# Opening loads of a two-layer hybrid kernel issued on three DMA queues, and its parameter columns made two blocks later

## The reference

```python
for i in range(DEPTH):                                   # DEPTH = 2
    mod_l = split(silu(c) @ w_mod[i] + b_mod[i], 6)      # six vectors of 1024, latent
    mod_c = split(silu(c_ctx) @ w_mod[i] + b_mod[i], 6)  # the same for the context
    uc = modulated_norm(xc, norm1_w[i], mod_c[0], mod_c[1]) @ w_in[i]
    yc, ssd_ctx, ml_ctx = token_mixers(uc, p, ssd_zero, ml_zero, not last)
    ul = modulated_norm(xl, norm1_w[i], mod_l[0], mod_l[1]) @ w_in[i]
    yl, _, _ = token_mixers(ul, p, ssd_ctx, ml_ctx, True)
    xl = xl + mod_l[2] * (yl @ w_out[i])
    xl = xl + mod_l[5] * hier_moe(modulated_norm(xl, norm2_w[i], mod_l[3], mod_l[4]), p)
    # the context rows likewise, in layer 0 alone
return rmsnorm(xl, final_norm_w)
```

## Time and profile before

| what | value |
|---|---|
| median of 3 runs | 1335.11 us (1330.76 to 1339.67) |
| the profiled execution's own time | 1335.6 us |
| its span, from first to last instruction | 1333.7 us |
| mean granted TensorE clock | 0.946 of full speed |
| TensorE busy with matmuls | 1177.0 us, 88% of the span |
| VectorE, ScalarE, GpSimd busy | 605.7, 306.7, 133.2 us |
| bytes moved | 321.40 MB, 241 GB/s in the mean |

### The profile page before, as it was taken

How to read it: one execution, slowest core, us unless ns; L and a number is a source line. 1 busy time by engine, 2 the same in 40 slices (tenths; PEclk the granted TensorE clock), 3 DMA queues, 4 the chain that set the end, 5 groups by cost and what they waited for, 6 DMA issues and landing times. The chain is left out here.

```text
span 1333.7 us, 19484 instructions
## 1 busy us (share of the span) xinstructions
PE 1177.0 (88%) x7596; PEld 774.2 (58%) x7596; DVE 605.7 (45%) x1233; ACT 306.7 (23%) x623; POOL 133.2 (10%) x144
## 2 busy tenths in 40 slices
PE   6799999999899989999778689998889899988882
PEld 3444547977678754555444466466768655545551
DVE  4423996038963642343111256964294533332223
ACT  4201212265352202131111232122542200000001
POOL 0000000000000012222121100000000112222220
PEclk9899999999889989999888899998999899998997
DMA  8653333337651679999999745441574879999982
GB/s 273 191 175 96 96 111 95 93 125 232 204 192 37 248 249 384 393 387 366 386 380 377 273 144 168 128 139 50 171 254 180 352 282 387 386 387 393 403 342 114
DMA packets 146421, 321.40 MB, mean 241 GB/s; under 512 B 28217, under 2 KB 111222, under 8 KB 121368
## 3 DMA queue, kind: packets, MB, share of 16 engines
q1 hardware_dynamic: 134840, 304.08, 63.1%
q0 software_dynamic: 11392, 15.79, 3.6%
q10 hardware_dynamic: 96, 0.26, 0.0%
HBM read 320.32 MB, written 21.23 MB: 256 GB/s over the span
## 5 line engine op out<-in xcount | busy, mean ns | idle before, releaser
L649 PE MATMUL bank<-hT,ring 128*128 128x512 f32 (+1 forms) x544 | 205.7, 535 | 1.8 <-DVE hT L1772 1.8
L649 PE MATMUL bank<-ring,hT 128*128 128x256 f32 (+1 forms) x928 | 182.3, 352 | 7.1 <-DVE ysum L1776 3.6
L649 PEld LDWEIGHTS bank<-ring,hT 128*128 128x128 f32 x928 | 155.6, 195 | 26.5 <-issue 5.2
L649 PE MATMUL bank<-chain,qkT 128*64 128x256 f32 (+1 forms) x792 | 149.9, 394 | 12.7 <-DMA chain<-in_moe_w_up 5.4
L649 PEld LDWEIGHTS bank<-hT,ring 128*128 128x128 f32 x544 | 103.2, 192 | 98.0 <-issue 91.6
L1776 DVE TENSOR_TENSOR ktok<-ktok,bank 64x256 f32<-64x256 f32 x65 | 27.5, 423 | 279.7 <-ACT ktok L1390 215.8
L1390 ACT ACTIVATE ktok<-bank 64x256 f32<-64x256 f32 (+2 forms) x79 | 32.1, 407 | 349.0 <-PE bank L649 273.4
L649 PEld LDWEIGHTS bank<-chain,qkT 128*64 128x64 f32 (+1 forms) x792 | 89.1, 156 | 33.7 <-issue 12.3
L1323 POOL DMA_INDIRECT pair_rows<-hyT,ysum x65 | 65.7, 1010 | 385.8 <-ACT hyT L1390 197.9
L649 PE MATMUL bank<-ring,qkT 128*64 128x256 f32 x528 | 87.2, 404 | 11.9 <-DMA ring<-in_moe_w_up 8.1
L649 PEld LDWEIGHTS bank<-ring,qkT 128*64 128x64 f32 x528 | 53.5, 145 | 28.5 <-issue 9.7
(11 more groups left out here) (291 smaller groups left out, 1698.9 us busy)
## 6 DMA issues: line engine op xcount, KB each, us to landing
ring<-in_w_mod SPq DMA_DIRECT2D x40, 1024.0 KB
chain<-in_moe_w_up SPq DMA_DIRECT2D x23, 1024.0 KB
ring<-in_w_in SPq DMA_DIRECT2D x22, 1024.0 KB
chain<-in_moe_w_down SPq DMA_DIRECT2D x19, 1024.0 KB
chain<-in_moe_w_gate SPq DMA_DIRECT2D x19, 1024.0 KB
ring<-in_moe_w_down SPq DMA_DIRECT2D x18, 1024.0 KB
ring<-in_moe_w_up SPq DMA_DIRECT2D x17, 1024.0 KB
ring<-in_moe_w_gate SPq DMA_DIRECT2D x16, 1024.0 KB
```

What stands on the lines that cost most here:

```text
L649: return nc.tensor.matmul(o, a, b, start=s, stop=e, **k)
```

## The change

`fetch` and the functions that call it take the issuing engine as an argument. The opening loads are dealt out to three queues:

- SyncE keeps the large ones, in their order: `first_pair(0)`, x, `first_pair(1)`, `first_pair(2)`, `first_single(6)`, `first_single(7)`, then `inproj_weights(0)` with nothing small in between.
- ScalarE issues ten at the start of its program: the three of `cond_in` and the seven of `hidden_parameters(0)`.
- GpSimd issues the other 52 at the start of its own: `tap_parameters(0)` (2), the modulation biases (2), the norm weights (2), dft (1), `parameters(0)` (36), the constants (5) and `router_parameters(0)` (4).

TensorE's `small_columns()` in layer 0 moves from behind the transposes to behind the first `channel_major("hy", 6, 0, ...)`. VectorE's program is as before. The same bytes are loaded to the same places. Layer 1 issues its small loads on SyncE as before.

```diff
             loading = [inproj_weights(l) for l in range(DEPTH)]
...
-                    fetch("cond_in", cond_v[:, :, 0], A["c"][0].rearrange("(p k) -> p k", k=KB))
-                    fetch("cond_in", cond_v[:, :, 1], A["c_ctx"].rearrange("(p k) -> p k", k=KB))
-                    fetch("cond_in", ident[:, :], A["const_ident"])
-                    hidden_parameters(0)
-                    tap_parameters(0)
                     first_pair(0)
-                    fetch("x_in", x_v[:, 0:2, :], A["ctx"][0].rearrange("(t p) d -> p t d", p=P))
+                    fetch(sp, "x_in", x_v[:, 0:2, :], A["ctx"][0].rearrange("(t p) d -> p t d", p=P))
...
                     first_pair(1)
                     first_pair(2)
-                    fetch("dft_in", dft[:, :], A["const_dft"])
                     first_single(6)
-                    for layer in range(DEPTH):
-                        fetch("mod_bias_in", bmod_v[:, layer], A["b_mod"][layer].rearrange("(m p k) -> p m k", m=6, k=KB))
-                    norm_weights(0)
                     first_single(7)
...
-                        if (l, name, q) == (0, "hy", 0):
-                            parameters(0)
-                            router_parameters(0)
-                        if (l, name, q) == (0, "hy", 1):
-                            for const, t in (("gsel", gsel), ("mask", ysum[:, 1024:1024 + 2 * P]), ("keep", keep),
-                                             ("iom", iom), ("inv", inv)):
-                                fetch("consts_in", t[:, :], A["const_" + const])
...
@@ def _(pe):
                         for s in range(2):
                             input_columns(k, s)
-                    small_columns()
                     pe.wait_ge(*due(("h1T", l, 0)))
...
                 for q in range(3):
                     channel_major("hy", 6, q, lambda blk: n0)
+                    if l == 0 and q == 0:
+                        small_columns()
...
@@ def _(pool):
+            tap_parameters(pool, 0)
+            for layer in range(DEPTH):
+                fetch(pool, "mod_bias_in", bmod_v[:, layer], A["b_mod"][layer].rearrange("(m p k) -> p m k", m=6, k=KB))
+            norm_weights(pool, 0)
+            fetch(pool, "dft_in", dft[:, :], A["const_dft"])
+            parameters(pool, 0)
+            for const, t in (("gsel", gsel), ("mask", ysum[:, 1024:1024 + 2 * P]), ("keep", keep), ("iom", iom), ("inv", inv)):
+                fetch(pool, "consts_in", t[:, :], A["const_" + const])
+            router_parameters(pool, 0)
...
@@ def _(act):
+            fetch(act, "cond_in", cond_v[:, :, 0], A["c"][0].rearrange("(p k) -> p k", k=KB))
+            fetch(act, "cond_in", cond_v[:, :, 1], A["c_ctx"].rearrange("(p k) -> p k", k=KB))
+            fetch(act, "cond_in", ident[:, :], A["const_ident"])
+            hidden_parameters(act, 0)
             act.wait_ge(*due(("cond_in",)))
```

## The result

| | before | after |
|---|---|---|
| median (20 runs each) | 1333.71 us (1329.66 to 1339.67) | 1340.60 us (1338.72 to 1346.44) |
| profiled execution, its span | 1335.6, 1333.7 | 1340.38, 1338.6 |
| mean granted TensorE clock | 0.946 | 0.947 |

The ratio after to before is 1.0056, 95% interval 1.0045 to 1.0066: the change costs 7.5 us (6.0 to 8.8). The forecast was 4 us less. The time lies within the range given, on the wrong side of no change.

A forecast was written before the change was run, and what follows sets the result against it. TensorE, busy for 88% of the span, was taken as the bound. Gains of 8.3 us less a 4 us delay gave 4.3 us off the profiled 1335.6: forecast 1331 us, range 1322 to 1353.

The forecast's parts named there:

- the term d: ScalarE's ten opening loads land later beside the large stream, delaying TensorE's filter chain by 4 us, bounds 0 and 6.5.
- Steps 1 to 4: On TensorE up to the second Hyena chunk: gains 3.7, 0.8, 3.8 and 0, sum 8.3 us, at most 10.4.
- step 3: The 6.04 us wait for the last router row before the projection: starting when hT is there gains 3.8 us.
- step 1: Gaps of 1.64 and 2.08 us, before modulation 2 and for the last single load, vanish: gain 3.7 us.
- T: Theory of the experiments, not the prediction: the delay is ScalarE's queue's piece count times a turn beside the stream.
- 0.37 to 0.70 us each: Issue times of ScalarE's ten opening loads, taken as SyncE's were, so the last starts near 6.4 us again.
- Rival B: SyncE's issues hold up ScalarE's: tenth starts near 21 us, 14.7 later; 1342, or 1346 with the load; chance 0.15.
- GpSimd's queue: Its 52 opening DMAs: last router row lands at 48.1, needed at 74.1; hidden up to 3.5 ns a piece.
- rival A: GpSimd makes pieces in software, so the last router row stalls TensorE 22 us (1353) or 67 (1398); chance 0.25.
- shares, and arrives later: Skill's rule on the opening loads: the hidden group shares DMA engines with the weights; without it, 4 us better.
- One for one to the end: An advance or delay at the start of the projection reaches the kernel's end in full; SyncE's loads wait for TensorE.

The follow-up runs named there:

- experiment 9: The kernel after with small_columns back at its old place ahead of the projection, loads as changed; 1339.92 us, ratio 1.0041.
- experiment 3: The kernel after with ScalarE's ten loads put back at the head of SyncE's queue, ahead of the large stream; 1331.02 us, ratio 0.9979.
- experiment 6: The kernel after with SyncE's first large loads waiting until the hidden group has landed; 1330.92 us, ratio 0.9989.
- e10: The kernel e8 with the taps moved from ScalarE's queue to SyncE's, behind the hidden group and ahead of the stream; 1327.31 us, ratio 0.9954.
- experiment 11: The kernel e8 with ScalarE's five loads put on SyncE's queue ahead of the stream; 1325.46 us, ratio 0.9939.
- experiment 1: The kernel after with c and c_ctx stored one behind the other, 128 runs of 32 bytes each, not 1024 pieces; 1335.57 us, ratio 1.0016.
- experiment 7: The kernel of experiment 1 with all 52 GpSimd loads, taps included, waiting for TensorE's first product; 1335.90 us, ratio 1.0024.
- experiment 5: The kernel after with c_ctx loaded once more on ScalarE's queue, in 1024 pieces of 4 bytes into a spare tile; 1349.44 us, ratio 1.0134.
- e2: The kernel after with GpSimd's 50 loads behind the taps waiting for TensorE's first product; 1342.24 us, ratio 1.0061.
- e4: The kernel before with only small_columns moved behind the first Hyena chunk, every load where it was; 1329.09 us, ratio 0.9969.
- e8: After, with c/c_ctx contiguous, hidden group heading SyncE's queue, dft on SyncE, taps on ScalarE, GpSimd's rest behind modulation 1; 1324.95 us, ratio 0.9941.

## Why the prediction was wrong, point by point

The step that failed is the one that priced ScalarE's ten loads, the term d: forecast 4 us, measured 16.3. The gains came out near their sum, in part by luck.

**Steps 1 to 4, the gains: right.** The waits of 1.64 and 2.08 us are gone, the mod vector behind the second takes 1.13, and nothing waits for a router row. To the start of the projection it is 43.60 us from the first product, before 53.20: 9.6 gained where the sum had 8.3. Of the 1.3 more, 0.7 arise before the products on the ones (19.31 us behind the first product, 20.04 before); the rest I did not follow. The first chunk gives 0.7 back, 16.74 against 16.08, with a granted clock of 0.50 after the idle 2.54 us: nothing was to be taken there, and nothing was. Sum 8.8 for 8.3. What step 3 did not see is that the queues alone would have earned it (experiment 9). And step 1 had some luck: a filter chain that starts 16.3 us late gives the weights as much more time. In experiment 3, with its first product at 10.60, they are waited for before modulation 4 (2.00 us), and in experiments 6, 10 and 11 there are such waits of 4.21, 2.31 and 3.58.

**What comes, d: the term that failed.** Forecast 4 us with bounds of 0 and 6.5; measured 16.3. It had two mistakes. The price came from a row of a load in one piece, as the latency of one transfer; the ten loads are 2776 packets. And they were taken for "a small load beside a busy stream", by their bytes, where the engines share by turns. The pieces of GpSimd's loads were counted, from the code, to 7450; those of ScalarE's were not. Had they been, and had a turn of one packet each been taken for granted, the rows of before would have given the size: a piece of the stream is 2 KB by the code or 2.7 KB as it now shows, at 367 GB/s over 16 engines 0.09 to 0.12 us, and 2626 pieces are 164 turns an engine, 15 to 19 us. From 2 us on that is a landing at 17 to 21 and a d of 9 to 13, still short of 16.3 but beyond the 8.3 gained, so with the sign right.

The runs bear the cause out in five ways, each beyond the 2 us by which first products of the same loads differ: fewer pieces (first product 5.0 us earlier), more pieces (9.65 us later), no stream (13.7 earlier), the same pieces ahead of the stream (13.8 earlier), and GpSimd's queue away (5.0 earlier than with fewer pieces alone). They don't bear out one price for a piece. Packets of SyncE's, GpSimd's and ScalarE's queues, and 4 us / (ScalarE's / 16):

| stretch | after | a turn, us | experiment 1 | a turn, us |
|---|---|---|---|---|
| 4 to 8 us | 335, 121, 124 | 0.52 | 418, 65, 124 | 0.52 |
| 8 to 12 us | 283, 274, 277 | 0.23 | 215, 209, 208 | 0.31 |
| 12 to 16 us | 481, 415, 475 | 0.135 | 331, 323, 316 | 0.20 |

Turns are longest while GpSimd's decays pass (0.43 MB in 121 packets from 4 to 8 us of after) and short once it sends small pieces. T expected 13 in experiment 1, and 19.38 came, for two reasons. Of after's 2776 packets some 1000 had passed by 4 us, so with 1792 taken away 760 were left to pass behind that time in place of 1772, 63 an engine less and not 112; and their turns were longer, (19.38 − 4) / (760 / 16) = 0.32 us in the mean for (24.40 − 4) / (1772 / 16) = 0.18. With GpSimd's queue held back (experiment 7, 762 left) the mean was 0.22.

**"0.37 to 0.70 us each" for the issues: wrong by 4.4 us.** Two issues took 3.02 and the next two 3.49, because the queue held a thousand pieces that hardly moved. In experiment 1 they took 1.33 and 2.03, in experiment 6, with the pieces but without the stream, 1.19 and 1.27.

**Rival B: the right place and time, the wrong cause.** It named a first product after 20 and 1342. The first product was at 24.40 and the time 1340.6. But its mechanism, SyncE's issues in ScalarE's way, is not what the runs show: with SyncE's program untouched, experiment 1 brings the issue back to 7.01. What is left for it is at most 7.01 − 6.39 = 0.6 us. Whoever had stopped at the first product would have called B confirmed.

**GpSimd's queue and rival A: hidden, as forecast.** GpSimd's 52 issues, two views of its timeline:

```profile
9.95 0.50 POOL L381 DMA_DIRECT2D prow<-in_hy_skip  x1
10.44 0.50 POOL L381 DMA_DIRECT2D gcolp<-in_ssd_dt_bias  x1
...
28.20 0.89 POOL L381 DMA_DIRECT2D rw<-in_exp_router_w  x1
...
29.62 0.55 POOL L381 DMA_DIRECT2D rb<-in_exp_router_b  x1
```

Most stand 0.50 us apart (0.85 taken), and the last lands at 29.62 + 6.3 = 36, needed at 85 (or at 67 in experiment 9). A load of 1024 pieces takes 0.39 us longer than one of a few: 0.4 ns a piece, far from the 3.5 from which a stall would begin. Rival A falls. The count of 7450 pieces was also no count of packets: GpSimd's queue has 13424 packets in after and 11392 in before, 2032 more, while SyncE's lost 134840 − 124102 = 10738, of which 2776 went to ScalarE's. So the loads that were 7962 packets on SyncE's queue are 2032 on GpSimd's. In the trace's DMA records, the gate columns' 1024 pieces of 48 bytes are 16 packets of 3072 bytes there. On ScalarE's queue each piece of 4 bytes stayed a packet of its own. No run puts c and c_ctx on GpSimd's.

**The Trainium skill** (DMA: Bandwidth & Descriptors, Issuing engines are not separate DMA queues) was read in the prediction as "shares, and arrives later". The rule that sizes it is in the Trainium skill too (DMA: Bandwidth & Descriptors, Queues, rings and completion order): each DMA engine goes round between the queues for which it has work, a packet from each. The trace agrees from 8 us on, with 283, 274 and 277 packets of three queues in 4 us of after and 331, 323 and 316 in experiment 1; from 4 to 8 us of after it does not, with 335, 121 and 124. The page puts a typical packet at some 9 to 17 descriptors (one descriptor is one contiguous piece); on ScalarE's queue it was one here: 1024 more pieces in experiment 5 are 3912 − 2872 = 1040 more packets.

**One for one to the end: borne out, within the noise.** The start of the second Hyena chunk in each profile (before: 78.31) against the time:

| kernel | first product | second chunk | against before | time against before (95%) |
|---|---|---|---|---|
| after | 24.40 | 85.79 | +7.5 | +7.5 (6.0 to 8.8) |
| e1 | 19.38 | 81.52 | +3.2 | +2.1 (0.4 to 4.0) |
| e2 | 24.37 | 85.15 | +6.8 | +8.1 (5.5 to 10.7) |
| e3 | 10.60 | 76.32 | −2.0 | −2.8 (−5.3 to −0.3) |
| e4 | 8.18 | 72.65 | −5.7 | −4.1 (−6.3 to −1.9) |
| e5 | 34.05 | 93.85 | +15.5 | +17.9 (13.5 to 22.4) |
| e6 | 10.66 | 75.82 | −2.5 | −1.5 (−3.6 to 0.8) |
| e7 | 14.39 | 79.91 | +1.6 | +3.2 (0.7 to 5.7) |
| e8 | 7.80 | 67.93 | −10.4 | −7.9 (−10.5 to −5.2) |
| e9 | 26.60 | 86.28 | +8.0 | +5.5 (3.2 to 7.6) |
| e10 | 6.08 | 69.41 | −8.9 | −6.1 (−8.7 to −3.6) |
| e11 | 7.53 | 68.75 | −9.6 | −8.1 (−11.3 to −4.9) |

The signs are kept. Of the losses, after, e2, e5 and e7 show all or more; e1 and e9 show two thirds. Of gains above 5 us the medians show 70 to 85%. Each interval but e10's and e9's holds the value of its row, and those miss it by 0.2 and 0.4 us. A second chunk is read from a single profile each, and a single execution scatters by more than these effects: e4's profiled one took 1336.53 us, the longest of its twelve, with the second chunk 5.7 us ahead. So this does not settle whether a little of a gain is lost later.

## What to carry to other kernels

Before a small load is put on SyncE's or ScalarE's queue beside a large stream on another, count its pieces: per DMA engine, pieces times the time of one packet from each of the other queues is what it takes, and the load's own bytes have little part in it. Here that was 0.135 to 0.15 us a piece while GpSimd sent small pieces, and 0.2 to 0.5 while it sent its long ones, so the count gives the sign and the order of size, not the microsecond. What is needed first goes ahead of the stream, in the stream's own queue if need be; what is needed later goes on the other queue, and behind a wait. And look at how the destination tile is interleaved: one axis the other way round took 1792 of 2872 packets away (5.0 us of the first product, 5 us of the time).

## What the hardware showed that I had not expected

- Two queues that both have packets waiting were served by count and not by bytes: 464 packets with 1.47 MB and 465 with less than 0.01 MB in the same 4 us (experiment 5). It did not hold in the first microseconds (212 and 38 from 4 to 6 us of after).
- The same loads were 7962 packets on SyncE's queue and 2032 on GpSimd's.
- A queue whose pieces don't move holds up its own engine's issues: with 1024 pieces more ahead of it the identity's took 12.07 us (experiment 5). Without them it took 0.68, 5.68 or 7.04 (after, experiments 2 and 9), and 0.68 when the stream was held back (experiment 6).
- GpSimd issued 52 direct DMAs in a row, most of them 0.50 us apart, and 1024 pieces cost it only 0.39 us more.
- The granted clock at the start of the projection differs behind the same idle time. TensorE idles 2.54 us in after and 2.55 in experiment 11; busy time by stretch (as Rows 2), two stretches of after and then two of experiment 11, from the start of each projection:

```profile
68.00:70.00 2.00, 2.00 (x3) 0.97 (x4) 0.00 (x0) 0.00 (x0) 0.00 (x0) 0.50 0.00 0
72.00:74.00 2.00, 2.00 (x4) 0.83 (x3) 0.00 (x0) 0.00 (x0) 0.00 (x0) 0.61 0.00 0
...
53.00:55.00 2.00, 1.28 (x3) 0.68 (x4) 0.62 (x1) 0.00 (x0) 0.00 (x0) 1.00 1.16 277
55.00:57.00 2.00, 2.00 (x6) 0.95 (x5) 0.00 (x0) 0.00 (x0) 0.00 (x0) 1.00 1.03 220
```

In after it stayed at 0.50 (1.2 GHz) for over 4 us and the first chunk took 16.74 us; in experiment 11 it stayed at 1.00 (2.4 GHz) and the chunk took 13.97. That is up to 2.8 us between kernels that otherwise do the same there, and no run here tells what decides it.
